# Part of each top-16 of a PEER layer computed by GpSimd, one step ahead, in place of VectorE

## What is computed

```python
s = jnp.einsum('nhpd,hpkd->nhpk', q, keys_f)          # 128 tokens, 8 heads, 2 halves, 128 keys
sv, si = lax.top_k(s, PEER_TOPK)                       # 16 best keys of each half
cand = sv[:, :, 0, :, None] + sv[:, :, 1, None, :]     # 16 x 16 sums
cidx = si[:, :, 0, :, None] * PEER_KEYS + si[:, :, 1, None, :]
fv, fi = lax.top_k(cand.reshape(n, 8, 256), PEER_TOPK) # 16 best pairs
eidx = jnp.take_along_axis(cidx, fi, axis=-1)          # their expert numbers
ue, ve = u_tab[eidx], v_tab[eidx]                      # two rows of 1024 floats per expert
act = gelu(einsum('nhkd,nd->nhk', ue, xb))
y = einsum('nhk,nhkd->nd', softmax(fv) * act, ve)
```

## Time and profile before

| | us |
|---|---|
| median of 3 runs | 4439.63 |
| span of the profiled execution, first to last instruction | 4442.9 |
| VectorE busy | 2697.7 |
| GpSimd busy | 2434.6 |
| TensorE matmul busy | 2228.0 |
| ScalarE busy | 1066.2 |

### The profile page before, as it was taken

One profiled execution on the slowest core, in us unless ns is written; L12 is line 12 of the kernel. 1 busy time (PEld: TensorE's weight loads), 2 busy tenths in 40 slices (PEclk: granted clock), 3 DMA queues, 4 the chain that ended last, 5 costly groups with the idle time before them and its releaser, 6 DMA issues.

```text
span 4442.9 us, 39715 instructions
## 1 busy us (share of the span) xinstructions
PE 2228.0 (50%) x11298; PEld 1070.2 (24%) x11298; DVE 2697.7 (61%) x6959; ACT 1066.2 (24%) x3546; POOL 2434.6 (55%) x2564
## 2 busy tenths in 40 slices
PE   4668656667925333333563298535753333333333
PEld 3544344334502100001430034403420000000000
DVE  1555866876455576764557554475566766767672
ACT  0122323332321122221132212221332122222221
POOL 0034534545554576775367443475467676777774
PEclk7879677668957655665776598767875556565555
DMA  5788888889999999999899987899999999999997
GB/s 172 243 281 311 306 292 315 307 289 358 386 374 371 384 409 409 409 409 368 317 397 409 369 304 278 325 409 354 357 373 409 409 409 401 401 405 399 406 403 302
DMA packets 576969, 1580.07 MB, mean 356 GB/s; under 512 B 49898, under 2 KB 237258, under 8 KB 576626
## 3 DMA queue, kind: packets, MB, share of 16 engines
q0 software_dynamic: 368640, 1342.34, 78.1%
q1 hardware_dynamic: 185650, 214.79, 14.3%
q10 hardware_dynamic: 22464, 20.46, 1.3%
HBM read 1551.21 MB, written 26.18 MB: 355 GB/s over the span
## 4 chain that ended last, share of the span: by engine, by line
DMA 32%; PE 18%; POOL 12%; issue 10%; DVE 8%; ACT 2%; SPq 0%; POOLq 0%; ACTq 0%; DVEq 0%
DMA v_ring<-in_peer_v_dram,idx_v 14%; POOL v_ring L827 8%; DMA u_ring<-in_peer_u_dram,idx 7%; PE ps_box L957 7%; PE ps_v L888 6%; POOL u_ring L817 5%; DMA w_slots<-in_w_mod_dram 4%; DVE u_ring L1626 3%; PE ps_box L1107 1%; DMA w_slots<-in_w_out_odd_dram 1%; DMA w_slots<-in_peer_keys_dram 1%; DMA w_slots<-in_w_in_odd_dram 1%; PE ps_box L928 1%; PE ps_box L1089 1%; DMA xa<-XM 1%
## 5 line engine op out<-in xcount | busy, mean ns | idle before, releaser
L1626 DVE CUSTOM_DVE_ANT_0 u_ring<-u_ring,h_cur 128x1024 f32<-128x1024 f32 x1280 | 1532.7, 1217 | 625.8 <-DMA u_ring<-in_peer_u_dram,idx 608.7
L817 POOL DMA_INDIRECT u_ring<-in_peer_u_dram,idx x1280 | 1216.3, 950 | 1174.1 <-DVE act_v L1626 619.0
L888 PE MATMUL ps_v<-v_ring,w_diag 128*32 128x512 f32 x5120 | 1017.0, 934 | 1499.2 <-DMA v_ring<-in_peer_v_dram,idx_v 1344.1
L827 POOL DMA_INDIRECT v_ring<-in_peer_v_dram,idx_v x1280 | 1218.1, 952 | 815.9 <-PE ps_v L888 450.2
L888 PEld LDWEIGHTS ps_v<-v_ring,w_diag 128*32 128x32 f32 x5120 | 196.1, 147 | 2228.0 <-issue 1584.4
L957 PE MATMUL ps_box<-HT,w_slots 128*128 128x128 f32 (+2 forms) x1792 | 479.7, 431 | 67.6 <-DMA w_slots<-in_w_in_odd_dram 32.6
L1245 ACT ACTIVATE w_v<-w_tok 32x4 f32<-32x4 f32 x1280 | 265.5, 207 | 797.3 <-DVE w_tok L1684 766.3
L957 PEld LDWEIGHTS ps_box<-HT,w_slots 128*128 128x128 f32 x1792 | 298.3, 212 | 256.5 <-issue 157.9
L1255 ACT ACTIVATE idx_v<-idx 32x4 uint32<-32x4 uint32 x1280 | 265.4, 207 | 239.3 <-PE ps_v L888 224.5
L1261 ACT ACT_TABLE_LOAD x79 | 101.4, 1283 | 380.8 <-DVE act_v L1626 367.3
L1107 PE MATMUL ps_box<-w_slots,CAT 128*128 128x256 f32 x640 | 160.3, 414 | 64.2 <-DMA w_slots<-in_w_out_odd_dram 40.7
(11 more groups left out here) (164 smaller groups left out, 2227.4 us busy)
## 6 DMA issues: line engine op xcount, KB each, us to landing
w_slots<-in_w_mod_dram SPq DMA_DIRECT2D x48, 1024.0 KB, 9.3
w_slots<-in_peer_wq_dram SPq DMA_DIRECT2D x48, 1024.0 KB, 13.6
u_ring<-in_peer_u_dram,idx POOLq DMA_INDIRECT x1280, 12.2
v_ring<-in_peer_v_dram,idx_v POOLq DMA_INDIRECT x1280, 12.2
w_slots<-in_w_in_odd_dram SPq DMA_DIRECT2D x16, 1024.0 KB, 16.6
w_slots<-in_w_in_even_dram SPq DMA_DIRECT2D x14, 1024.0 KB, 8.9
w_slots<-in_w_out_even_dram SPq DMA_DIRECT2D x12, 1024.0 KB, 11.7
w_slots<-in_w_out_odd_dram SPq DMA_DIRECT2D x12, 1024.0 KB, 21.9
```

The costliest lines, as they stand in the source:

```text
L817: pool.indirect_dma_start(out=u_ring[:, k % NU, :], out_offset=None, in_=u_rows, in_offset=bass.IndirectOffsetOnAxis(ap=idx[:, h % 2, k:k ...
L827: pool.indirect_dma_start(out=v_ring[:, k % NV, :], out_offset=None, in_=v_rows, in_offset=bass.IndirectOffsetOnAxis(ap=idx_v[:, h % 2, k: ...
L888: last = nc.tensor.matmul(ps_v[QUARTER * q:QUARTER * q + QUARTER, 512 * half:512 * half + 512], w_diag[:, c % GROUPS, q, :], v_ring[:, (r ...
L1626: nc.vector.tensor_tensor_reduce(u_ring[:, k % NU, :], u_ring[:, k % NU, :], h_cur[:, :], 1.0, 0.0, ALU.mult, ALU.add, act_v[:, h % 2, k:k ...
```

## The change

`topk` on VectorE ends with the one-hot rows, and signals them with a new semaphore `chosen_done`. The products, the sums, the expert number and the store into `idx` go to GpSimd as a function `decode`, which then signals `topk_done`. GpSimd calls `decode` for step i+1 inside `step` i, ahead of its third group of u gathers (c = 2), and `decode(0, 0)` ahead of all. The sum over 16 is now three additions of halves (8, 4, 2 wide) and one that leaves the result in `e01`. The last two VectorE instructions become three on GpSimd. VectorE's next `topk` waits until GpSimd has read the tiles of the one before (`topk_done` at least i), ScalarE's `load_s` waits for `chosen_done`, and the wait for `idx_v` moves to GpSimd.

```diff
@@ block.gpsimd
+            def decode(seg, h):
+
+                i = seg * 8 + h
+                l = seg // 5 if isinstance(seg, int) else seg.loop.lo // 5
+                wait(pool, chosen_done, i + 1)
+                for j in range(2):
+                    last = nc.gpsimd.tensor_tensor(onehot[:, j], onehot[:, j],
+                                                   sif[:, j, :].unsqueeze(1).to_broadcast([P, 16, 16]), ALU.mult)
+                chain(last)
+                for n in (8, 4, 2):
+                    chain(nc.gpsimd.tensor_tensor(onehot[:, :, :, 0:n], onehot[:, :, :, 0:n], onehot[:, :, :, n:2 * n], ALU.add))
+                chain(nc.gpsimd.tensor_tensor(e01[:, :, :], onehot[:, :, :, 0], onehot[:, :, :, 1], ALU.add))
+                chain(nc.gpsimd.tensor_scalar(e01[:, 0, :], e01[:, 0, :], float(KEYS), float(l * EXPERTS), ALU.mult, ALU.add))
+                chain(nc.gpsimd.tensor_tensor(e01[:, 0, :], e01[:, 0, :], e01[:, 1, :], ALU.add))
+
+                wait(pool, idx_v_done, i - 1, "idx")
+                nc.gpsimd.tensor_copy(idx[:, h % 2, :], e01[:, 0, :]).then_inc(topk_done, 1)
+
             def step(seg, h, first=False):
                 i = seg * 8 + h
                 wait(pool, topk_done, i + 1)
                 for c in range(GROUPS):
+                    if c == 2 and (h < 7 or not (isinstance(seg, int) and seg == 9)):
+                        decode(seg + (h + 1) // 8, (h + 1) % 8)
                     for k in range(4 * c, 4 * c + 4):
                         gather_u(i, h, k)
@@
+            decode(0, 0)
             for i in range(16):
                 step(i // 8, i % 8, first=i == 0)
@@ block.scalar
             def load_s(i, h):
 
-                wait(act, topk_done, i - 1)
+                wait(act, chosen_done, i - 1)
@@ block.vector
             def topk(seg, h):
 
                 i = seg * 8 + h
                 wait(dve, s_landed[h % 2], 64 * seg + 16 * (h // 2) + 16)
+                wait(dve, topk_done, i)
                 wait(dve, exp_done, i - 1, "topk")
@@
-                chain(last)
-                for j in range(2):
-                    last = nc.vector.tensor_tensor(onehot[:, j], onehot[:, j],
-                                                   sif[:, j, :].unsqueeze(1).to_broadcast([P, 16, 16]), ALU.mult)
-                chain(last)
-                chain(nc.vector.tensor_reduce(e01[:, :, :], onehot[:, :, :, :], AX, ALU.add))
-                chain(nc.vector.scalar_tensor_tensor(e01[:, 0, :], e01[:, 0, :], float(KEYS), e01[:, 1, :], ALU.mult, ALU.add))
-
-                wait(dve, idx_v_done, i - 1, "idx")
-                nc.vector.tensor_scalar(idx[:, h % 2, :], e01[:, 0, :], float(l * EXPERTS), None, ALU.add).then_inc(topk_done, 1)
+                last.then_inc(chosen_done, 1)
```

More of the change, by code:

```diff
@@ L280, in build @@
         s_landed = [sem("s_landed0"), sem("s_landed1")]
+        chosen_done = sem("chosen_done")
         topk_done = sem("topk_done")
@@ L296, in build @@
         act_chain = sem("act_chain")
+        pool_chain = sem("pool_chain")
         box_ready = [sem(f"box_ready{i}") for i in range(BOXES)]
@@ L809, in _ @@
             per_seg = {(dots_done, ""): (128, 1 - NU), (vsum_done, ""): (32, -7), (topk_done, ""): (8, 1),
-                       (idx_v_done, ""): (8, 0)}
+                       (idx_v_done, ""): (8, 0), (idx_v_done, "idx"): (8, 0), (chosen_done, ""): (8, 2)}
+            chain = Chain(pool, pool_chain)
             u_rows = T["peer_u"].rearrange("l e d -> (l e) d")
@@ L845, in _ @@
             with Segments(pool, 2, 4, per_seg) as seg:
+                chain.restart()
                 for h in range(HEADS):
@@ L1224, in _ @@
                       (vsum_done, "spread"): (32, -4), (w_done, "gelu"): (8, -2), (w_done, "exps"): (8, -2),
-                      (dots_done, ""): (128, 0), (dots_done, "h"): (128, 128), (negmax_done, ""): (8, 2), (topk_done, ""): (8, 1),
+                      (dots_done, ""): (128, 0), (dots_done, "h"): (128, 128), (negmax_done, ""): (8, 2), (chosen_done, ""): (8, 1),
                       (h_landed, ""): (16, 32), (x_new, ""): (1, 0)}
@@ L1608, in _ @@
             per_seg = {(h_ready, ""): (1, 1), (s_landed[0], ""): (64, 32), (s_landed[1], ""): (64, 32), (exp_done, "topk"): (8, 1),
-                      (exp_done, "weigh"): (8, 0), (vsum_done, "end"): (32, 0), (idx_v_done, "idx"): (8, 1),
+                      (exp_done, "weigh"): (8, 0), (vsum_done, "end"): (32, 0), (topk_done, ""): (8, 2),
                       (gelu_done, ""): (8, 0), (w_v_done, ""): (8, 0), (w_v_done, "weigh"): (8, -1), (vsum_done, "diag"): (32, -9), (seg_landed, ""): (32, 0), (acc_free, ""): (1, 0),
@@ L1648, in topk @@
                 i = seg * 8 + h
-                l = seg // 5 if isinstance(seg, int) else seg.loop.lo // 5
                 wait(dve, s_landed[h % 2], 64 * seg + 16 * (h // 2) + 16)
+                wait(dve, topk_done, i)
                 wait(dve, exp_done, i - 1, "topk")
```

## The result

| | before | after |
|---|---|---|
| median, us | 4439.95 (4 runs) | 4537.45 (4 runs, 4527.52 to 4547.3) |
| ratio | | 1.0217, 95% interval 1.0199 to 1.0235 |
| profiled span, us | 4442.9 | 4539.9 |

What follows compares the result with a forecast made beforehand. DMA engines pace rows-only steps at 42.3 us; the decode makes GpSimd the bound. +105 (42 steps) - 18 (VectorE's gain in dense stretches) + 3 (start) = +90 us, 4530 us; own range 4455 to 4620, 8 in 10: 4412 to 4650.

Steps and rivals of the forecast that it cites:

- What bounds the kernel before: Rows-only stretches: DMA engines set 42.3 us a step, with GpSimd 2.1 to 2.6 us behind.
- D: Time the decode's nine instructions add to GpSimd's step: 2.6 us arithmetic plus 2.4 us pauses, 5.0 us; likely 3.5 to 7.
- The time that the prediction worked out from that ratio: With the skill's ratio of 1.96, D would be 7.5 us and the time about 105 us above the forecast.
- GpSimd's own pace: GpSimd's step without the decode: 39.8 us, since two VectorE two-input instructions beside gathers go away; otherwise 40.2.
- The steps that count: 42 steps in the three rows-only stretches, each 2.5 us longer (44.8 against 42.3): 105 us.
- Dense stretches: Steps beside dense work: VectorE's shorter top-16 gains about 18 us on the chain, GpSimd's decode costs nothing.
- The cover named in the prediction: Dense stretches: decode-delayed gathers cost nothing, since VectorE has up to eight landed rows in stock, 9.8 us of work.
- Cheap decode: Decode below 2.1 us fits GpSimd's spare time; only VectorE's 25 us gain is left, 4415 us; chance 0.14.
- Balance: D of 2.7 to 3.2 us costs 13 to 25 us, cancelled by VectorE's 18: 4440 us; chance 0.09.
- Slow arithmetic: GpSimd's decode takes around 9 us, by its length or contention with VectorE: 4695 us; chance 0.09.
- Waits in dense stretches: GpSimd waits 2.7 us for one-hot rows, delaying gathers in 38 steps: 103 us more, 4630 us; chance 0.08.
- The moved wait for `idx_v`: Now on GpSimd ahead of 8 u gathers, about 5 us earlier; the list is ready 24 us before: costs nothing.

Runs made afterwards that it cites:

- half rows: Half the bytes in every gather, in both kernels: 4126.81 us for the kernel before, 4346.07 us for the changed one.
- the last three: Changed kernel with products and sum over 16 back on VectorE, GpSimd keeping only the last three instructions: 4433.23 us, ratio 0.9985.
- the sums: Changed kernel with products back on VectorE, sums and the rest on GpSimd in pieces, each waited for ahead of the next piece: 4439.66 us, ratio 0.9995.
- the whole decode with late waits: Changed kernel, decode in eight pieces between u gathers, each waited for ahead of the next piece, not of the gather: 4473.23 us, ratio 1.0074.
- the doubled decode: Changed kernel with unused arithmetic of the decode's shapes added on GpSimd behind every decode: 4745.91 us, ratio 1.0679.
- the run of idle arithmetic in the first 16 steps: Kernel before plus unused arithmetic of the decode's shapes on GpSimd in the first 16 steps only: 4455.23 us, ratio 1.0031.
- two versions in pieces: Changed kernel, whole decode in pieces between u gathers: waits ahead of the next gather 4609.15 us, waits ahead of the next piece 4473.23 us.
- the idle arithmetic on GpSimd: Kernel before plus unused arithmetic of the decode's shapes on GpSimd in every step, VectorE's top-16 whole: 4555.72 us, ratio 1.0258.
- VectorE's work cut: Kernel before with the product and the sum over 16 left out on VectorE, nothing added to GpSimd: 4424.9 us, ratio 0.9965.

## Why the prediction was right

The mechanism was right: in rows-only stretches the decode's time adds to GpSimd's row of gathers, and GpSimd takes over the pace from the DMA engines. But several errors of the sum, named below, cancel, and to that extent the closeness of 90 to 97 us is luck.

**What bounds the kernel before** was right: half rows show the DMA engines as its bound and GpSimd 2.4 us behind, where the prediction had 2.1 to 2.6 us.

**D** was 4.64 us where 5.0 were estimated, but its two terms were both off and nearly cancelled. The arithmetic lasts 3.9 us, not 2.6; the waits between the instructions cost mostly 0.08 us each, not 0.30, and only the start of the gather behind the decode is late (0.56 in place of 0.30 us). GpSimd's groups over the whole span, against VectorE's 424, 288 and 198 ns:

```profile
L840 POOL TENSOR_TENSOR onehot<-onehot,sif 128x256 f32<-128x256 f32 x160 | 116.5, 752 | 251.4 <-DVE onehot L1691 250.0
...
L844 POOL TENSOR_TENSOR onehot<-onehot 128x128 f32<-128x128 f32 x80 | 37.0, 463 | 6.3
...
L850 POOL CAST idx<-abf 128x16 uint32<-128x16 f32 x80 | 16.1, 201 | 22.4 <-ACT idx_v L1281 14.6
```

GpSimd took 1.8 times VectorE's length at 256 elements, 1.6 times at 128, the same at 16. The Trainium skill (GPSIMD Engine Reference, Performance versus the Vector engine) gives 1.96 for 2048 elements; the direction agrees, and at these sizes the factor is smaller. The time that the prediction worked out from that ratio, 105 us above its forecast, did not come.

**GpSimd's own pace** was taken at 39.8 us, from single gathers, because VectorE's two products would go away; with the 40.2 that the groups gave it would have been right (40.3 with half rows, 45.0 - 4.64 = 40.4 in the changed kernel). The DMA engines' pace in whole segments is 42.7, not 42.3. Both errors are 0.4 to 0.5 us a step and cancel; D was 0.36 us smaller, so 2.3 us a step were measured where 2.5 were forecast.

**The steps that count** were taken as 42 at the full price, 105 us. 42 steps at 2.3 us would be 94 to 97. The segments from 2 on except 5 hold 90 us, dense parts of them included. Segment 6 gave only 3.5.

**Dense stretches** is the step that failed. Forecast: -18 us from VectorE, +3 at the start, nothing for GpSimd, together -15. Measured: segments 0, 1 and 5 together +7 us, of which 4.2 arose ahead of the first top-16, so +3 to +7. VectorE's gain is real (15 us for 1.45 us), but GpSimd's time is not free there: arithmetic of the decode's length costs 0.85 us a step, 13.6 us in the first 16 steps alone. The cover named in the prediction, VectorE's stock of eight rows, is incomplete. In the traces 15 us too much in the rows-only term and 22 us too little in this one leave the 7 us between 90 and 97; with the 4.2 us taken out it is 18 us too little.

**The rivals.** Cheap decode: excluded by D; its own rule (no loss below 2.1 us) is borne out by the last three at 1.15 us and the sums at 1.7. Balance: D is outside its 2.7 to 3.2 us. Its price was too low, too: the whole decode with late waits has D = 3.0 and VectorE's full saving, and takes 4473 us, not 4440; 42 x 0.6 = 25 us of the 33 are its pace of 43.3, the rest lies elsewhere. Slow arithmetic: D would have to be 9 for 4695 us; the doubled decode has 8.63 and gives 4746 us, so this price was too low as well, by what GpSimd's time costs outside the 42 steps. Waits in dense stretches: `chosen_done` was waited for 10 times in the whole span, 250 us of which 232 are the start, ahead of any gather; the other nine are 1.3 to 6.4 us each, 18 us together. The moved wait for `idx_v`, which the prediction had put at nothing, held GpSimd once, for 14.6 us at 297 us in segment 0. In the trace with the last three it held GpSimd for 19.0 us at the same place, and that version is no slower than the kernel before, so it can't cost much. No run takes the waits away alone; the run of idle arithmetic in the first 16 steps, which has neither, shows that the length costs without them.

## What to carry to other kernels

An engine that shows 55% busy can be 6% from being the bound, as GpSimd here, 2.4 us in 42.7: add up what it must do in one period with the pauses between its instructions, and compare with the period, before giving it work. Halving the bytes of the transfers is a cheap way to see the next bound behind the DMA engines and how far it is. Where work must go between DMA issues of the same queue, keep the wait for it away from the next issue: here the place of the waits was worth 136 us between two versions in pieces.

## What the runs showed of the hardware

A gather's time on GpSimd hardly depends on its bytes: 128 rows of 4 KB take 0.95 us in the mean, 128 rows of 2 KB 0.96 us, and the row of them has a floor of 1.24 to 1.26 us a gather (pace 40.3 us with half rows). The 0.30 us between gathers isn't lost to arithmetic: an instruction that no gather waits for starts 0.01 us after a gather's end in the decode's timeline (3741.13 us), and in the pieces with late waits the next gather starts 0.16 us after it.

The two engines do hold each other up. VectorE's diagonal (two SBUF inputs) went from 288 ns to this:

```profile
L1661 DVE TENSOR_TENSOR w_diag<-w_v,eye 128x128 f32<-128x128 f32 x320 | 101.2, 317 | 142.0 <-ACT w_v L1271 125.7 <-PE ps_v L914 16.3
```

With the idle arithmetic on GpSimd it was 309 ns, with VectorE's work cut and none on GpSimd 287 ns. The Trainium skill (SBUF — State Buffer, Who interferes with whom) says that such instructions contend with GpSimd's reads; the traces agree, and the size is 9 us of VectorE's busy time over 320 instructions. How much of the 97 us that is, no run shows.

The gathers are held up too, in the kernel before as well. All 13 that start while VectorE adds or multiplies two SBUF tiles at the end of a segment (1.22 to 1.29 us each) end 0.80 to 0.82 us after that instruction's end and last up to 1.89 us in place of 0.94; the gather in the earlier trace rows is one of them.
